# Hybrid decoder layer on one core: the remaining projections by spans of 512 tokens, with seven products of half sums in place of eight past the first span

## What is computed

```python
xn = rmsnorm(x, norm_gain)
h = jnp.einsum('btd,dn->btn', xn, w_in)
cb, cc, cu, cz, q, k, v, az, iq, ik, iw, gc, ga = split_cols(h)
conv_y, conv_state = short_conv(cc * cu, conv_prev, conv_w)
y_conv = cb * conv_y * jax.nn.silu(cz)
y_attn = attend(q, k, v, iq, iw, ik) * jax.nn.silu(az)   # top 256 keys by an indexer, softmax, ALiBi
m = (jax.nn.sigmoid(gc) * jnp.einsum('btc,cd->btd', y_conv, w_up_conv)
     + jax.nn.sigmoid(ga) * jnp.einsum('bta,ad->btd', y_attn, w_up_attn))
x = x + jnp.einsum('btd,de->bte', m, w_out)
```

## Time and profile before

| | |
|---|---|
| median of 3 runs | 2865.04 us (2860.5 to 8133.02) |
| the profiled execution, its own time | 2864.7 us |
| its span, first to last instruction | 2862.9 us |
| PE busy | 2663.6 us, 93% of the span |
| DVE busy | 1932.3 us, 67% |
| ACT busy | 832.8 us, 29% |
| POOL busy | 49.0 us, 2% |
| mean granted clock of TensorE | 0.974 |

### The profile page before, as it was taken

How to read it: one execution, slowest core, us unless ns; L and a number is a source line. 1 busy time by engine, 2 the same in 40 slices (tenths; PEclk the granted TensorE clock), 3 DMA queues, 4 the chain that set the end, 5 groups by cost and what they waited for, 6 DMA issues and landing times. The chain is left out here.

```text
span 2862.9 us, 31303 instructions
## 1 busy us (share of the span) xinstructions
PE 2663.6 (93%) x11650; PEld 1481.7 (52%) x11650; DVE 1932.3 (67%) x3938; ACT 832.8 (29%) x1363; POOL 49.0 (2%) x65
## 2 busy tenths in 40 slices
PE   7987998999999999999999998899999868999988
PEld 5743444454444545454545454555555546676653
DVE  5219899987797989887989997126995014454443
ACT  4222233322323233333333333311221342231210
POOL 0000000000000000000000000100000100000000
PEclk9998999999999999999999999899999989999999
DMA  7111111111111111111111010131225749453307
GB/s 213 32 37 35 43 42 41 31 46 35 40 45 35 36 38 30 41 38 37 33 35 35 26 43 24 52 115 72 103 104 126 220 193 292 156 187 108 129 30 30
DMA packets 212680, 215.33 MB, mean 75 GB/s; under 512 B 76720, under 2 KB 199216, under 8 KB 208880
## 3 DMA queue, kind: packets, MB, share of 16 engines
q1 hardware_dynamic: 203824, 153.13, 18.6%
q0 software_dynamic: 7072, 60.18, 6.8%
q10 hardware_dynamic: 1632, 0.01, 0.1%
HBM read 157.56 MB, written 55.72 MB: 74 GB/s over the span
## 5 line engine op out<-in xcount | busy, mean ns | idle before, releaser
L787 PE MATMUL attn_ps_r<-xnT,early 128*128 128x424 f32 (+2 forms) x2464 | 993.1, 543 | 30.5 <-ACT early L638 15.7
L115 DVE TENSOR_SCALAR_CACHE_REDUCE early<-early 128x384 uint8<-128x384 f32 (+13 forms) x462 | 681.8, 1476 | 11.5
L787 PEld LDWEIGHTS attn_ps_r<-xnT,early 128*128 128x128 f32 x2464 | 442.9, 191 | 441.0 <-issue 423.5
L1089 PE MATMUL samp_ps_r<-xnT,early 128*128 128x424 f32 (+1 forms) x800 | 288.2, 523 | 6.1 <-PEq L89 6.1
L657 ACT ACTIVATE attn_probT<-attn_ps_p 128x512 f32<-128x512 f32 (+1 forms) x288 | 151.9, 571 | 407.2 <-PE attn_ps_p L832 407.0
L1646 PE MATMUL merge_ps_y<-merge_w_out,merge_merged 128*128 128x512 f32 (+1 forms) x544 | 235.0, 592 | 1.2 <-DVE merge_merged L1775 1.2
L1089 PEld LDWEIGHTS samp_ps_r<-xnT,early 128*128 128x128 f32 x800 | 153.2, 192 | 138.9 <-issue 138.3
L715 DVE SCALAR_TENSOR_TENSOR early<-attn_relu,early 128x512 f32<-128x512 f32 (+3 forms) x266 | 182.1, 684 | 31.4 <-ACT attn_relu L674 4.1
L638 ACT ACTIVATE early<-attn_ps_r 128x424 f32<-128x424 f32 (+1 forms) x130 | 67.9, 523 | 427.8 <-PE attn_ps_r L787 426.5
L817 PE MATMUL attn_ps_s<-kT,qT 64*128 64x512 f32 (+3 forms) x640 | 163.9, 592 | 25.6 <-DVE early L744 18.5
L832 PE MATMUL attn_ps_p<-ident,prob 128*128 128x128 f32 x1088 | 156.8, 283 | 25.8 <-ACT prob L693 25.8
(11 more groups left out here) (231 smaller groups left out, 2366.0 us busy)
## 6 DMA issues: line engine op xcount, KB each, us to landing
rest_t<-early SPq DMA_DIRECT2D x144, 212.0 KB, 1.9
early<-in_w_in SPq DMA_DIRECT2D x104, 256.0 KB, 3.4
early<-in_x_prompt SPq DMA_DIRECT2D x16, 512.0 KB, 4.0
merge_x<-in_x_prompt SPq DMA_DIRECT2D x8, 1024.0 KB, 5.0
out_y_prompt<-merge_y POOLq DMA_DIRECT2D x16, 512.0 KB, 4.1
rest_t<-early SPq DMA_DIRECT2D x36, 208.0 KB, 2.1
merge_ga<-rest_t SPq DMA_DIRECT2D x7, 1024.0 KB, 10.9
merge_gc<-rest_t SPq DMA_DIRECT2D x7, 1024.0 KB, 9.4
```

The lines of the kernel that those rows point to most:

```text
L115: self.v.done(self.nc.vector.tensor_scalar(self.hits, self.x, limit, None, op, ALU.add, accum_out=self.count))
L787: ins = nc.tensor.matmul(ps_r[:, 0:width], w_rest[:, n % 2, k, :], c.xnT[:, k, t0:t0 + width], start=(k == 0), stop=(k == KC - 1))
L1089: ins = nc.tensor.matmul(ps_r[:, i % 2, 0:width], w_rest[:, (slot0 + j) % 2, k, :], c.xnT[:, k, t0:t0 + width], start=(k == 0), stop=(k == ...
```

## The change

**Order of tokens.** The samples stand at the front of `xnT` (columns 0 to 63) and the prompt behind them. The token axis of the rest is cut in a first span of 64 + 512 tokens and three further spans (`SPAN`) of 512.

**First span.** Each of the 36 blocks is done as before, in two items of 288 tokens (`PART`, kind "whole", 8 matmuls each). After each pair of blocks GpSimd forms four sums of quarters of the pair's weights in place (`sum_weights`, four TENSOR_TENSOR of 128x512) and writes them to a new tensor `sums` in memory (1 MB a pair).

**Later spans.** For each pair of blocks and each span, a "group" of seven items (kind "part") stands in place of 32 matmuls of width 512: each item is 4 matmuls of width 256, of a weight quarter or sum (128 columns by half the model width) with a half of the tokens or a sum of halves (Winograd's form of Strassen's product). Part of the recombination is done by accumulating in PSUM (items outside `OPENS` add to what the bank holds); three of the results go to `part`, and GpSimd adds them to `result` (three TENSOR_TENSOR of 128x256 a group, `combine`). The four token sums of a span (128x1024 each, `difference`) are formed by GpSimd over tokens that are no longer needed. There are 18 pairs x 3 spans = 54 groups, of which 34 are in the prompt stage and 20 in the sample stage.

**Queries** go by 256 tokens (`QB`) in place of 512: the norm stage computes the samples' queries and attention's first 256 (L476 and after it, width 320 = 64 + 256 in one matmul), and the prompt stage has 56 query items of 8 matmuls of width 256.

**Loads.** Weights go through a ring of eight buffers of half a block (256 KB, two DMAs each). Each of the seven items of a group has its own load, from `w_in` or from `sums`. A ring slot that held a pair's weights comes free when the pair's sums are out.

**Planning.** The filler is counted in whole items, in slots of `fill`; `split` gives at most one item ahead of a head's transposes, half of the others before the next scores and half after. `PAIRS_OF_TILE` and `GROUPS_OF_TILE` take the place of `REST_LOADS`. The columns of filler that each tile T gets (its matmuls times their width) and the number of item ends with no other PE work behind them:

| tile | 2 | 3 to 6 | 7 to 9 | 10 | 11 | 12 | 13 | 14 | 15 | 16 |
|---|---|---|---|---|---|---|---|---|---|---|
| columns before | 8192 | 25088 each | 41984 each | 41984 | 41984 | 54784 | 50688 | 50688 | 50688 | 0 |
| columns after | 17408 | 26624 each | 35840 each | 36864 | 44032 | 51200 | 51200 | 47104 | 35840 | 14336 |
| open ends before | 0 | 4 in all | 7 in all | 1 | 1 | 1 | 0 | 0 | 0 | 0 |
| open ends after | 1 | 6 in all | 5 in all | 10 | 16 | 20 | 16 | 15 | 8 | 1 |

(Two more open ends after are in tiles 0 and 1.)

**Sample stage.** `replicate` and the write of the bias move from POOL's queue to SP's, behind the last store of the rest. POOL's gathers stand among its `combine` steps.

```diff
-REST_LOADS = [0, 0, 0, 1, 1, 1, 1, 2, 2, 2, 2, 2, 3, 3, 3, 3, 0]
+PAIRS_OF_TILE = [0, 0, 1, 2, 2, 2, 2, 3, 3, 3, 0, 0, 0, 0, 0, 0, 0, 0]
...
+WEIGHTS = [(0, 0), (0, 1), 0, 3, 2, 1, (1, 1)]
...
+ORDER1 = (3, 5, 0, 2, 4, 6, 1)
+ORDER2 = (0, 3, 2, 5, 4, 1, 6)
+OPENS = (0, 1, 3)
...
+def operands_of(c, group):
+
+    b11, b12, b21, b22 = tokens_of(c, group)
+    t1, t2, t3, t4 = sums_of(c)
+    return [b11, b21, t2, t1, t3, b22, t4]
...
+                        for l in plan.free[n]:
+                            kind, of, i, _ = plan.loads[l]
+                            if kind == "block":
+                                sp.wait_ge(w_sums_out[i // 2 % 2], 16 * (i // 4 + 1))
+                            else:
+                                sp.wait_ge(rest_done, n + 1)
+                            load(l + RING)
...
+                    a11, a12, a21, a22 = [slot_of(c, load + x) for x in range(4)]
+                    pool.wait_ge(rest_done, n + 1)
+                    nc.gpsimd.tensor_tensor(a22, a21, a22, ALU.add).then_inc(w_summed, 1)
...
+                    pool.dma_start(a["sums"][pair], src[:]).then_inc(w_sums_out[pair % 2], 16)
...
-            ins = nc.tensor.matmul(ps_r[:, 0:width], w_rest[:, n % 2, k, :], c.xnT[:, k, t0:t0 + width],
-                                                   start=(k == 0), stop=(k == KC - 1))
...
+                            if n:
+                                pe.wait_ge(rest_kept, n)
...
+                                    ins = nc.tensor.matmul(ps_r[:, 0:HALF], w, operands_of(c, item.of)[item.i][:, k, :],
+                                                           start=(k == 0 and item.i in OPENS), stop=(k == 3),
+                                                           skip_group_check=item.i not in OPENS)
...
-                pool.wait_ge(rest_done, len(steps))
+                combine(RESTS[2], RESTS[3])
+                pool.wait_ge(rest_done, in_all)
+                for s in range(2):
+                    pool.wait_ge(rest_stored[s], 32 * sum(g % 2 == s for g in groups))
                 keys(2)
                 values(1)
-                pool.wait_ge(added, 1)
-                replicate(2)
```

591 lines of the change are left out of this document (394 added, 197 removed).

## The result

The changed kernel takes **3020.3 us** (median of 4 runs, 3011.1 to 3031.4) against 2863.7 of the kernel before: ratio 1.055, 95% interval 1.050 to 1.060. It is 157 us slower, where 26 us less were forecast, and lies outside the range of 2783 to 2905. One of the four executions of the kernel before took 8133 us; the ratio leaves it out. The profiled execution took 3031.4 us, 11 above the median; its span is 3029.6.

A forecast was written before the change was run, and what follows sets the result against it. PE was taken to bound the norm stage's queries, PE and DVE together the prompt, PE and then data the sample stage. Terms -31 + 26 - 21 = -26 against 2864.7 gave 2839 us, range 2783 to 2905.

The forecast's parts named there:

- Norm stage, -31: Norm stage's queries: fall from 55.8 us to 24.8, all of it counting, 31 us saved.
- PE's work, -19: Prompt stage: PE's products fall from 902.8 us to 883.6, 19 us saved.
- Ends of items, +34: Prompt stage: 100 open ends at 0.56 us each wait for ACT's copies, 56 us against 22, 34 us lost.
- Where the work goes, -6: Prompt stage: columns moved between tiles; 20 us not had in tile 15, 16 and 10 hidden in tiles 16 and 2.
- Coarser filler and exps, +12: Prompt stage: uncut items of 1.7 us lie beside a head's exps; bounds 0 and +168, 12 us lost.
- ACT late behind the exps: Prompt stage rival: PE waits 1.5 us more a head for exps, 2911 us in all; chance 0.12.
- Weight sums, +5: Prompt stage: GpSimd's sums and their write make weight slots come free tightly, 5 us lost.
- weight sums late: Prompt stage rival: each of 16 pairs 2 to 5 us late, 2866 to 2914 us; chance 0.13.
- loads of the sample stage too slow: Sample stage rival: at 150 GB/s each group takes 15.7 us, +72, 2911 us; chance 0.05.
- GpSimd slows DVE: Prompt stage rival: GpSimd's sums conflict with DVE's two-input instructions, 11 to 35 us lost, 2850 to 2874; chance 0.13.
- Sample stage, products, -42: Sample stage: products fall from 283.8 us to 241.7, 42 us saved.
- Sample stage, the bias, +21: Sample stage's end: weighing starts 49 us after the last product, less 28 of covered key waits, 21 us lost.

The follow-up runs named there:

- the three edits together: Changed kernel with exps ahead of the copies, items spread inside their slots, and an item in every second index-score slot: 2934.4 us.
- light loads: Changed kernel with bias and replicas early on SP's queue, and weight loads of the sample stage's last 16 items cut to 16 columns: 3018.5 us.

## Why the prediction was wrong, point by point

**Norm stage, -31**: right. The queries take 7.36 and 17.45 us in the trace, 25 as forecast.

**PE's work, -19**: the price held (a step of 0.43 us); the saving lies under larger losses.

**Ends of items, +34**: the mechanism was right, 103 waits against 100 counted, and the size too small: 0.74 us an end and not 0.56, since I priced the idle time alone. Measured +27 shown + 70 x 0.27 = +46. I also read the longest wait of before as 0.7 us; the earlier trace rows has one of 0.9.

**Where the work goes, -6**: wrong on tiles. Tile 9 was to be 9 us shorter and is 2 longer, tile 11 ten longer and is 22, tile 16 eight longer and is 19. Tile 15, 150 forecast, is 155.

**Coarser filler and exps, +12**: this is the step that failed most. It cost 60 us shown, 75 with the hidden part. Two steps were wrong. I took it that one item of 1.7 us lies ahead of every head's transposes; 36 of the 64 heads have none, and 69.7 of the 85.8 us are theirs. And I wrote that "PE is most often behind DVE's maximum rather than ahead", and put the wait near its lower bound. The maximum was early, by 9.4 to 22.1 us in tiles 11 to 14; but ACT came to the exps only behind copies of items that PE was yet to compute. Before, an item of 5.68 us could be cut, so that its copy fell behind the exps, and part of it lay beside them. Exps ahead of the copies took 35 us off the wait and 52 off the stage; items cut again took 50 off the wait. The rival "ACT late behind the exps" had the wait and, by luck, its size (84 us, 2911), from an item that ends before the second exp; the missing items and ACT's order it did not have. I gave it 0.12.

**Index scores**: no term at all. Whole-item counting left these slots empty: +29 us shown, +40 with the hidden part (41 more waits). Filling every second slot took 28 of the 29 off, but the scores' wait for DVE gave 24 back. The order of instructions, which I had, shows it; I looked at one place in tile 12 only, behind the scores of attention.

**Weight sums, +5**: nothing. PE waited for no load in tiles 3 to 9, and the rival "weight sums late" is out. So is "loads of the sample stage too slow": 3 us of waits for them up to the last product.

**GpSimd slows DVE**, a rival at 11 to 35 us for the prompt: 18 us there with the sums shortened, as a part of the loss, and 13 in the sample stage. It also holds copies. Two waits of PE in the sample stage, 13.8 us, are for ACT, which waits for a sum of GpSimd. The one of 6.3 us is behind sums that took 5.0 to 9.2 us beside DVE's scan and the long instructions around it, where others of the size take 0.72; it is gone with shortened sums. The one of 7.5 us is behind a sum that stands in GpSimd's order behind eight gathers and its clearing of tiles; with shortened sums 6.3 us of it stay.

**Sample stage, products, -42**: 18 had. PE's products take 30 us less, their modelled ends included; 13.8 us of that go to the two waits for ACT and 2.9 to waits for loads.

**Sample stage, the bias, +21**: +65. The waits grew by 61 us shown, and PE's own work there takes 4 more. The replicas share the DMA engines with the gathers for 39 us and not for 15 + 12, and the second wait (24.9 us) stands behind ACT's order. I took the replicas' time from a row of GpSimd's queue, and they went to SP's.

What is open: about 17 of the 151 us of the prompt stage are in no wait that I counted (the granted clock is 0.97 there and was 0.98); 63 of the 151 stay with the three edits together; what an item ahead of every head's transposes would give by itself; and why replicas on SP's queue fill only half of the DMA engines.

## What to carry to other kernels

Filler that becomes finer in size but coarser in how it can be cut loses three times: each end costs a full restart, short slots get none, and so do the places where it was to cover a wait. Count these places in the plan before giving them a price. Look, for each instruction on the copying engine, at what stands ahead of it in its own order and whether that has been computed yet; an engine with 30% busy time can be the bound by order alone. Where PE is busy 94% of a stage, count every wait that a plan adds, at its full price from start to start, before the products that it saves.

## What was not expected of the hardware

A wait of PE for a copy between products costs 0.74 us where 0.47 are shown as idle (256 columns), and 0.84 where 0.57 are shown (264 columns). A GpSimd sum of 128x256 takes 0.72 us alone and beside DVE's search passes of 4.54 us, and 5.0 to 9.2 us while DVE runs the instructions behind the search: a compare of 64x4096, the scan and two-input instructions of that size. Each of these slow sums ended within 0.6 us of the DVE instruction beside it, and with the sums cut to 8 columns one still took 8.0 us there. DVE's two-input instruction of 512 columns takes 851 ns in place of 751 on average while GpSimd works, and the small two-input step of its search (434 times in the prompt) 202 in place of 159; with shortened sums they are at 751 and 160. A replicating read of one row of 16.6 KB to 64 partitions, two at a time, runs at 111 to 137 GB/s from SP's queue and at 225 from GpSimd's, with what is beside it. While PE waited in the sample tail its granted clock fell to 0.50 (the lower of its two levels, 1.2 of 2.4 GHz), as in the second row on light loads and from 2394 to 2420 us in the changed kernel, and the stage's mean is 0.89 against 0.96.
